# Feed-forward gate and up projections as Strassen block products, with three stretches per layer

## What is computed

```python
def swiglu(x, w_in, w_out):                 # w_in: 1024 x 5632, w_out: 2816 x 1024
    gate, up = jnp.split(x @ w_in, 2, axis=-1)
    return (jax.nn.silu(gate) * up) @ w_out

def macaron_layer(x, mixer, ...):
    x = x + FFN_HALF * rmsnorm(swiglu(rmsnorm(x, ffn1_pre_g), ffn1_w_in, ffn1_w_out), ffn1_post_g)
    x = x + rmsnorm(mixer(rmsnorm(x, mix_pre_g)), mix_post_g)
    x = x + FFN_HALF * rmsnorm(swiglu(rmsnorm(x, ffn2_pre_g), ffn2_w_in, ffn2_w_out), ffn2_post_g)
```

## Time and profile before

| what | value |
|---|---|
| device time, median of 3 runs | 3333.84 us (3322.33 to 3336.97) |
| span of the profiled execution | 3333.7 us |
| TensorE busy | 3161.7 us, 95% |
| VectorE (DVE) busy | 1652.0 us, 50% |
| ScalarE (ACT) busy | 1199.2 us, 36% |
| GpSimd (POOL) busy | 685.7 us, 21% |
| mean granted TensorE clock | 0.967 |
| read from HBM | 255.61 MB, 77 GB/s |
| chain that ended last | PE 83%, DVE 8%, ACT 4%, POOL 2% |

### The profile page before, as it was taken

The page is one execution under the profiler, slowest core; times in us unless marked ns, Lnnn a source line. Parts: engine busy times, 40 slices in busy tenths (PEclk is TensorE's granted clock), DMA queues, the critical chain, the costliest instruction groups (busy, mean ns, idle before and its releaser), DMA issues.

```text
span 3333.7 us, 43230 instructions
## 1 busy us (share of the span) xinstructions
PE 3161.7 (95%) x17800; PEld 2514.6 (75%) x17800; DVE 1652.0 (50%) x2636; ACT 1199.2 (36%) x2094; POOL 685.7 (21%) x579
## 2 busy tenths in 40 slices
PE   6999999899999999999789999999999999999998
PEld 3877677677777788877677788888888885588886
DVE  2155564436674534475654553446444525564344
ACT  3242264443263322342343432234222415542222
POOL 3234314334514000045221200000000243220000
PEclk8999999999999999999677999999999999999999
DMA  6213211221102332232000233232232230022322
GB/s 230 95 36 133 95 31 40 70 73 52 60 13 80 105 99 94 91 101 81 8 8 2 70 100 109 92 109 78 90 107 86 86 108 32 2 98 89 110 83 82
DMA packets 78740, 260.50 MB, mean 78 GB/s; under 512 B 8528, under 2 KB 11728, under 8 KB 77392
## 3 DMA queue, kind: packets, MB, share of 16 engines
q1 hardware_dynamic: 77680, 253.02, 23.5%
q0 software_dynamic: 864, 4.72, 0.4%
HBM read 255.61 MB, written 2.10 MB: 77 GB/s over the span
## 4 chain that ended last, share of the span: by engine, by line
PE 83%; DVE 8%; ACT 4%; POOL 2%; issue 1%; DMA 1%; SPq 0%; ACTq 0%; DVEq 0%; POOLq 0%
PE banks L363 81%; PE banks L372 2%; POOL w_lo L354 1%; DVE x_lat L708 1%; DVE w_lo L354 1%; DVE area L705 1%; DMA area<-in_w_mod 1%; ACT w_hi L344 0%; DVE small L2080 0%; POOL area L428 0%; DVE area L2029 0%; DVE area L636 0%; DMA w_raw<-in_l_ffn_w_in 0%; DVE area L546 0%; DVE w_late L354 0%
## 5 line engine op out<-in xcount | busy, mean ns | idle before, releaser
L363 PE MATMUL banks<-area,w_hi 128*128 128x512 f32 (+4 forms) x5980 | 1745.4, 375 | 28.6 <-POOL w_lo L354 13.0
L363 PEld LDWEIGHTS banks<-area,w_hi 128*128 128x128 f32 (+2 forms) x5980 | 1084.3, 188 | 277.8 <-issue 31.8
L363 PE MATMUL banks<-area,w_lo 128*128 128x512 f32 (+4 forms) x2990 | 1108.5, 372 | 0.0
L363 PEld LDWEIGHTS banks<-area,w_lo 128*128 128x128 f32 (+2 forms) x2990 | 561.9, 188 | 110.6
L363 PE MATMUL banks<-area,w_late 128*128 128x512 f32 (+2 forms) x2370 | 554.0, 384 | 8.1 <-DVE w_late L354 5.3
L344 ACT ACTIVATE w_hi<-w_raw 128x1024 fp32r<-128x1024 f32 (+2 forms) x353 | 341.3, 970 | 540.9 <-PE banks L363 405.6
L363 PEld LDWEIGHTS banks<-area,w_late 128*128 128x128 f32 (+1 forms) x2370 | 429.8, 188 | 108.4 <-DVE w_late L354 6.6
L363 PE MATMUL banks<-area,area 64*64 64x32 f32 (+11 forms) x4424 | 402.8, 316 | 64.9 <-DMA area<-in_w_mod 15.7
L363 PEld LDWEIGHTS banks<-area,area 64*64 64x64 f32 (+4 forms) x4424 | 309.0, 175 | 146.9 <-issue 59.8
L428 POOL TENSOR_TENSOR area<-area,area 128x512 f32<-128x512 f32 (+1 forms) x72 | 92.6, 1290 | 1379.3 <-ACT area L413 1377.8
L354 POOL TENSOR_TENSOR w_lo<-w_raw,w_hi 128x1024 fp32r<-128x1024 f32 (+1 forms) x124 | 284.8, 2299 | 403.5 <-ACT w_hi L344 403.4
(11 more groups left out here) (259 smaller groups left out, 2474.9 us busy)
## 6 DMA issues: line engine op xcount, KB each, us to landing
w_raw<-in_l_ffn_w_in SPq DMA_DIRECT2D x176, 512.0 KB, 3.4
w_raw<-in_l_ffn_w_out SPq DMA_DIRECT2D x128, 384.0 KB, 3.0
w_raw<-in_w_in SPq DMA_DIRECT2D x66, 512.0 KB, 3.5
w_raw<-in_w_mod SPq DMA_DIRECT2D x32, 512.0 KB, 4.4
w_raw<-in_w_qkv SPq DMA_DIRECT2D x24, 512.0 KB, 3.5
w_raw<-in_l_w_in SPq DMA_DIRECT2D x22, 512.0 KB, 3.5
w_raw<-in_w_out SPq DMA_DIRECT2D x32, 320.0 KB, 2.9
area<-in_w_mod SPq DMA_DIRECT2D x8, 1024.0 KB, 16.6
```

Source lines behind the costliest of these rows:

```text
L363: return e.matmul(out, lhsT, rhs, start=first, stop=stop, skip_group_check=True)
```

## The change

For feature tiles 3 to 21 of each layer (19 of 22) the gate piece and the up piece are computed together, as one product of a 2 x 2 block matrix by a 2 x 2 block matrix: two blocks of output features (gate, up), two halves of the 1024 inputs (g0, g1 and u0, u1 are a piece's two halves of 512 columns), two halves of the 512 tokens. In place of eight block products there are seven, in the form that shares sums (Strassen-Winograd). Each is 4 blocks x 3 passes = 12 matmuls of 256 columns. Tiles 0 to 2 (`DIRECT = 3`) stay as they were.

- Combined weights: s1 = u0+u1, s2 = s1-g0, s3 = g0-u0, s4 = g1-s2, each 128 x 512, made by POOL out of the raw buffers for every tile, written where the low parts will stand, and then split into high and low like the rest. TensorE uses seven quarter pieces: g0, g1 ("plain"), s1, s2 ("s12"), s3, s4 ("s34"), u1 ("last"). "last" has a small buffer pair of its own.
- Combined activations t0 to t3 (128 x 1024 each) are made once per layer by DVE and split by ACT, DVE and POOL.
- Sums of the seven products: two 256-column PSUM quarters are copied to SBUF by ACT (`p1`, `u2`), and five additions of a quarter are done by DVE (c11, u4, c22, c12, c21). Scaling by the norm's root is then two DVE instructions from SBUF to SBUF (`scale`).
- The low part of "plain" is made by POOL, those of the other three by DVE.
- The raw buffers stay three. The gate piece's buffer is free after s4. The up piece's buffer is free after the low part of "last", and "last" of a tile stands in the order of the splits behind "plain" and "s12" of the next tile.
- Three stretches of 8, 8 and 6 tiles take the place of two halves of 11. `w_out` comes in 24 pieces in place of 32, and the output is added up over three stretches.

The diff, cut to its core:

```diff
-FFN_K = (6, 5)
+FFN_PHASES = ((0, 8), (8, 16), (16, 22))
+DIRECT = 3
...
+            if split and "ffn" in name and name.endswith("_w_in") and index >= 2 * DIRECT:
+                if index % 2 == 0:
+                    ents += [(n, "plain"), (n, "s12")]
+                    if ents[-3][1] == "s34":
+                        ents.append((ents[-3][0], "last"))
+                    ents.append((n, "s34"))
+                elif order[n + 1][0] != name:
+                    ents.append((n - 1, "last"))
+            elif split:
+                ents.append((n, "whole"))
...
+        def rest_to(q, e, limit, dve=False):
...
+                if kind == "last" and dve:
+                    q.wait_ge(*at("weights hi", m, kind))
+                    e.tensor_tensor(lo, raw_of(m + 1)[:, QUARTER:], hi.bitcast(f32), SUB).then_inc(
+                        *sig(name, "weights", m, kind))
+                    also("raw free", m + 1)
+                if kind in ("s12", "s34") and dve:
+                    q.wait_ge(*at("weight sums", m, "s34"))
+                    q.wait_ge(*at("weights hi", m, kind))
+                    e.tensor_tensor(lo, sums_of(m, kind), hi.bitcast(f32), SUB).then_inc(*sig(name, "weights", m, kind))
+                if kind in ("s12", "s34") and not dve:
...
+                    q.wait_ge(*at("raw", m + 1))
+                    slot_free(q, k)
+                    if kind == "s12":
+                        e.tensor_tensor(s1, u0, u1, ADD).then_inc(*sig("w_sums"))
+                        q.wait_ge(*last())
+                        e.tensor_tensor(s2, s1, g0, SUB).then_inc(*sig("w_sums", "weight sums", m, kind))
+                    else:
+                        e.tensor_tensor(s3, g0, u0, SUB).then_inc(*sig("w_sums"))
+                        q.wait_ge(*at("weight sums", m, "s12"))
+                        e.tensor_tensor(s4, g1, s2, SUB).then_inc(*sig("w_sums", "weight sums", m, kind))
+                        also("raw free", m)
...
+            def pe(self, q, e):
+                self.project.pe(q, e, lead=self.LEAD)
+                for p in range(len(FFN_PHASES)):
+                    units = self.units(p)
+                    for u in units:
+                        for name in ("p1", "p2", "p5", "p6"):
+                            self.product_pe(q, e, u, name)
+                        if u > units[0]:
+                            self.product_pe(q, e, u - 1, "p4")
+                        for name in ("p7", "p3"):
+                            self.product_pe(q, e, u, name)
+                    self.product_pe(q, e, units[-1], "p4")
+                    self.outs[p].pe(q, e)
...
+            def act(self, q, e):
...
+                    for u in units:
+                        unit_end = self.ent(u, "s34")
+                        more = u < units[-1]
+                        if more:
+                            round_to(q, e, unit_end + 1)
+                        q.wait_ge(*at(self.tag, "product", u, "p1"))
...
+                        e.activation(self.p1[u % 2], self.quarter(u, 0), ACT.Copy).then_inc(
+                            *sig("ffn_p1", self.tag, "p1", u))
```

More of the change, by code:

```diff
@@ L331, in round_weights, with round_to @@
         def round_weights(q, e, n, more=None):
-            while q.w <= ahead(n, more):
-                m = q.w
+            round_to(q, e, ahead(n, more))
+        def round_to(q, e, limit):
+            while q.w <= limit:
+                k = q.w
                 q.w += 1
[L336 to L344, removed]
@@ L1187, in __init__ @@
                     self.norm = Halved(name, gain, x_event, Area(pre_at))
+                self.norm.rs = self.norm.squares.rs = Area(RS_AT).take(T)
                 self.add = HalfAdd(name, lambda j, s: half_g[:, f, j:j + 1], y_sb, Area(post_at))
[L1189 to L1197 removed]
@@ L1198, in __init__ @@
-                self.first = self.halves[0][0].pieces[0]
+                self.first = piece_no[name + "_w_in", 0]
+                self.project = Project([(name + "_w_in", c) for c in range(2 * DIRECT)], P, self.norm, T)
+                Groups.made += -2 * DIRECT % 4
+                self.outs = []
+                for p, (j0, j1) in enumerate(FFN_PHASES):
+                    self.outs.append(ProjectOut(
+                        name, lambda m, p=p, n=j1 - j0: [(name + f"_w_out{p}", m, n)],
+                        [(self.a_hi[:, k, :], self.a_lo[:, k, :]) for k in range(j1 - j0)], T, y_sb, self.add.squares,
+                        lambda q, k, j0=j0: q.wait_ge(*at(name, "a", j0 + k)), add=p > 0, final=p == len(FFN_PHASES) - 1,
+                        free=lambda q, m, p=p: self.left_by_units(q, m, p), bank0=4 - 4 * self.bank_set(j1 - 1)))
@@ new lines, in scaled_act, with t_hi_act @@
+            def scaled_act(self, q, e):
+                for n in range(self.LEAD):
+                    q.wait_ge(*at("weights used", self.first + n, "whole"))
+                for k in range(4):
+                    e.activation(self.t[:, 0:3:2, k, :], X(k, 0).rearrange("p (h n) -> p h n", h=2), ACT.Identity,
+                                 scale=self.gain(k)).then_inc(*sig("t_scaled", self.tag, "t scaled"))
+                round_to(q, e, self.ent(DIRECT, "plain"))
+            def t_hi_act(self, q, e, i):
+                q.wait_ge(*at(self.tag, "t", i))
+                e.activation(self.t_hi[:, i], self.t[:, i], ACT.Copy).then_inc(*sig("t_hi", self.tag, "t hi", i))
@@ new lines, in silu_act, with a_hi_act @@
+            def silu_act(self, q, e, u):
+                q.wait_ge(*at(self.tag, "gate", u))
+                e.activation(self.sg[u % 2], self.sg[u % 2], ACT.Silu).then_inc(*sig("ffn_silu", self.tag, "silu", u))
+            def a_hi_act(self, q, e, u):
+                p = self.phase(u)
+                q.wait_ge(*at(self.tag, "product", u))
+                if p and u == FFN_PHASES[p][0]:
+                    q.wait_ge(*at(*self.outs[p - 1].finished()))
+                e.activation(self.a_hi[:, u - FFN_PHASES[p][0], :], self.a[u % 2], ACT.Copy).then_inc(
+                    *sig("a_hi", self.tag, "a hi", u))
```

451 lines of the change are left out of this document (337 added, 114 removed).

## The result

The changed kernel takes 3609.58 us (median of 4 runs, 3605.75 to 3614.26), the kernel before 3333.80 beside it (3322.33 to 3336.97): ratio 1.0831, 95% interval 1.0814 to 1.0848. It is slower by 276 us; forecast were 199 (3533 us, range 3375 to 3620). The profiled execution has a span of 3603.9 us, 270.2 more than before.

The account below looks back on a forecast made before the run. The prediction took the kernel before as bound by PE's matmul columns, the changed one by the ring of three raw buffers: 3333.7 + 151 (ring) + 48 (layer starts) = 3533 us, range 3375 to 3620.

Parts of the forecast that it names:

- PE at 0.35 us per three matmuls of 256 columns: PE's pace when fed: a tile takes 9.80 us in place of 11.20, 106 us less over 76 tiles.
- The ring: Raw buffers' loop of fetch, rounding, POOL's low part and sums, DVE's splits: 15.0 us a tile, +151 us; chance 0.64.
- DVE and POOL exclude each other: DVE instructions with two SBUF inputs and POOL's run one at a time: together 11.8 us a tile after overlaps.
- The rival with 11.8 us a tile as the only limit: Only DVE's and POOL's shared SBUF reads bind, raw pieces return in time: 3379 us; chance 0.12.
- the rival on the clock: PE's granted clock falls as PE idles, some 2 us a tile on 52 tiles: 3640 us; chance 0.12.
- 17 us a tile: Profile sign of the falling clock: tiles of 17 us at a clock of 0.7.
- The start of a layer: POOL's and DVE's extra work before the first combined tiles delays PE by 12 us a layer, +48 us; bounds 0 and 15.
- Ends of stretches: The last tile's root, product and split before the first output tile: nothing, at most 1 us.
- 108.5 + 44.8: 108.5 us was forecast for a stretch of 8 tiles, before 89.6; 44.8 us is one `w_out` stage.
- 8.6 us behind s12: End of a stretch: after the last tile's s12, PE has six products, 8.4 us, and small waits of 0.2.
- the ring's lower end: Fast end of the raw-buffer loop's own range: 3422 us, from 13.6 us a tile and layer starts of 4 us.

Follow-up runs that it names:

- in_psum: plain_dve with a tile's four quarter sums left in their PSUM banks, so a scaling reads a bank and the factor: 3357.25 us, ratio 1.0071.
- last_first: The changed kernel with "last" of a tile split ahead of the next tile's s12: 3509.64 us, ratio 1.0520.
- plain_dve: last_first with the low part of "plain" made by DVE instead of POOL, and "last" ahead of the up tile's scaling: 3405.89 us, ratio 1.0214.
- the pair of scalings: Two runs of the changed kernel, each leaving out one scaling a tile: the up tile's, 3553.67 us; the gate tile's, 3591.51 us.
- sums_first: The changed kernel with POOL making the four sums ahead of the low part of "plain": 3645.74 us, ratio 1.0928.
- the four edits of the layer's start: On in_psum: t3 combined earlier, 3365.53 us; splits ahead of direct tiles' work, 3376.79; combinations by four subtractions, 3355.72. The last on the changed kernel: 3592.26.

## Why the prediction was right, and where it was short

- **PE at 0.35 us per three matmuls of 256 columns**: right wherever it is fed. The gain is real: in_psum's stretch of eight is 4.4 us under that of before.
- **The ring, 15.0 us a tile**: 15.12 measured, link by link. last_first, plain_dve and the pair of scalings show that it is this chain: shortening it pays, the same work outside it hardly. No run gave the kernel a fourth raw buffer, which would have tested the ring most directly.
- **DVE and POOL exclude each other**: shown by 1223 against 686 ns and by sums_first. The rival with 11.8 us a tile as the only limit fell: it became nearly true (11.2) only after "last" and "plain" were moved, in plain_dve.
- **PE's busy time**: not forecast. It rose, since at the starts of stretches and after waits PE runs below full clock; that it lies mostly inside the ring's waits, as the rival on the clock had against itself, fits the period of 15.12, but no run separates it. That rival's 17 us a tile do not occur.
- **The start of a layer**: the step that was mis-sized. Forecast 12 us a layer, within 0 to 15. PE starts p1 of tile 3 at 1090.1 without a wait, so by the forecast's own terms the first "last" would start 9.8 us later, at 1100. It starts at 1117.1: 17 us, and 18 in each of the other three layers. I had left the last two low parts of t out of the path as needed late. They are, but the three are one run of 9.34 us on POOL, which blocks DVE's split (2.77 in place of 1.21), and the low part of "plain" of tile 4, a link of the ring, stands behind that run and starts when it ends, at 1107.05. ACT's rounding of that piece, held up by DVE's late product, had ended only 0.6 us before, so the low parts of t alone do not explain the delay. Its 5 to 6 us beyond the forecast are +23 us in four layers.
- **Ends of stretches**: "nothing, at most 1 us". The stretch of eight takes 158.1 us; without the forecast's 108.5 + 44.8 and the 1.1 us by which its six periods exceed 15.0, 3.7 us are left (3.7 to 4.5 in the other layers). Taken for all twelve ends that is +44 us. From the trace, at the end of the second stretch the last p4 ends 1.5 us later than 8.6 us behind s12, a wait of 0.92 us for c22 (L1597) included, and then PE waits 0.78 for a `w_out` split and 0.83 for `a_lo` (L1513): 3.2 of the 3.7. I had priced each one against the matmuls ahead of it, and several short ones stand in a row. No run took them away, so how they share the 3.7 stays open.
- **The period**: 0.12 us more on 52 tiles gives some 6. The three come to 73 us; the span's +270 exceeds the forecast +199 by 71.
- **Two slips of the forecast that change nothing**: its terms for the ring's lower end (13.6 us a tile, starts of 4 us) give 3428 and not 3422. And `w_out` comes in 16 pieces of 512 KB and 8 of 384 KB a layer, not in 24 of 512, so the changed kernel reads less, 251.41 MB in place of 255.61.

## What to carry to other kernels

Fewer matmul columns help only if what feeds them has a period below the new, shorter tile: write down the loop through the buffers (fetch, round, combine, split, free) and add it up before counting any engine's busy time. Work that is cheap on an idle engine is not cheap when it stands in that loop: here an order of two splits cost 100 us, and POOL's 2.4 us for what DVE does in 1.2, together with one more place in DVE's order, 104. And after an instruction is moved, look at what stands behind the one that now waits, on every queue; in three of the four edits of the layer's start PE's wait moved to ACT's copy of p1.

## What the runs showed of the hardware that was not expected

- Which of DVE and POOL is held up depends on which starts first: in sums_first POOL's 2.80 us instruction held a DVE split of 1.21 us for 3.03. An order on POOL that looks free can lengthen DVE's critical instruction by POOL's whole length.
- After PE had waited 9.09 us, at 1102.15, three matmuls of 256 columns started every 0.64 us in place of 0.35, until about 1110.8; the granted clock of 1100 to 1120 us was 0.73. The 30 matmuls in that time took 6.9 us in place of 3.5, so the wait cost PE some 3.4 us more behind it.
- A PSUM bank as one of DVE's two inputs costs nothing against SBUF, 686 against 692 ns, and takes the instruction out of the contention with POOL (1223 ns beside POOL's sums). As the output too it costs next to nothing: 425 ns for a quarter sum of 256 columns that stays in its bank (L1557 of in_psum), 416 for one that goes to SBUF (L1602).
